# Eight sums of squares in a decoder layer: one plain float32 product each, or two products of rounded parts

## The reference

```python
def rmsnorm(x, g):
    xf = x.astype(jnp.float32)
    y = xf * lax.rsqrt(jnp.mean(xf * xf, axis=-1, keepdims=True) + EPS)
    return (y * g.astype(jnp.float32)).astype(x.dtype)
...
mixed = jnp.sum(gates * proj, axis=2) @ w_mix_out[l]
x = x + rmsnorm(mixed, norm_post_mix[l])
h = rmsnorm(x, norm_pre_xa[l])
mem_n = rmsnorm(mem, mem_norm_g[l])
xa = cross_attention(h, mem_n, xa_wq[l], xa_wkv[l], xa_wo[l])
x = x + rmsnorm(xa, norm_post_xa[l])
h = rmsnorm(x, norm_pre_mlp[l])
ff = jnp.square(jax.nn.relu(h @ mlp_w1[l])) @ mlp_w2[l]
x = x + rmsnorm(ff, norm_post_mlp[l])
```

## Time and profile before

| what | us |
|---|---|
| median of 3 runs (lowest, highest) | 2530.48 (2529.13, 2532.38) |
| the profiled execution, its own time | 2537.36 |
| its span, first to last instruction | 2535.4 |
| busy: PE | 2490.1 (98%) |
| busy: DVE | 1527.9 (60%) |
| busy: POOL | 1240.2 (49%) |
| busy: ACT | 575.6 (23%) |

### The profile page before, as it was taken

One profiled execution on the slowest core, in us unless ns is written; L12 is line 12 of the kernel. 1 busy time (PEld: TensorE's weight loads), 2 busy tenths in 40 slices (PEclk: granted clock), 3 DMA queues, 4 the chain that ended last, 5 costly groups with the idle time before them and its releaser, 6 DMA issues.

```text
span 2535.4 us, 31059 instructions
## 1 busy us (share of the span) xinstructions
PE 2490.1 (98%) x11454; PEld 2053.9 (81%) x11454; DVE 1527.9 (60%) x1618; ACT 575.6 (23%) x777; POOL 1240.2 (49%) x957
## 2 busy tenths in 40 slices
PE   8999999999999999999999999999999999999997
PEld 5788888788888888888778787788788888888885
DVE  6896577587777776699586746652871231622123
ACT  4100444422222222111122214243431110211001
POOL 0433333322222222333676677745776666766663
PEclk9999999999999999999999999999999999999999
DMA  6322121211111112333664344432532232432323
GB/s 236 125 75 79 62 81 60 74 34 44 48 41 42 49 50 100 116 141 108 233 223 143 131 142 161 156 116 67 174 108 95 96 100 94 164 93 98 100 92 115
DMA packets 84883, 270.11 MB, mean 107 GB/s; under 512 B 7888, under 2 KB 9168, under 8 KB 83792
## 3 DMA queue, kind: packets, MB, share of 16 engines
q1 hardware_dynamic: 71760, 244.03, 28.1%
q10 hardware_dynamic: 13056, 25.17, 2.8%
HBM read 224.60 MB, written 44.56 MB: 106 GB/s over the span
## 4 chain that ended last, share of the span: by engine, by line
PE 86%; DVE 6%; issue 3%; POOL 2%; DMA 2%; ACT 2%; SPq 0%; ACTq 0%; POOLq 0%; DVEq 0%
PE ps L369 25%; PE ps L371 25%; PE ps L370 25%; PE xb L510 2%; PE ps L433 1%; POOL w_lo L1911 1%; DVE macc L770 1%; PE ps L423 1%; DMA w_raw<-wall 1%; POOL w_hi L1909 1%; PE xb L533 1%; PE xa L546 1%; PE xb L536 0%; PE xa L524 0%; PE xb L580 0%
## 5 line engine op out<-in xcount | busy, mean ns | idle before, releaser
L1911 POOL TENSOR_TENSOR w_lo<-w_raw,w_hi 128x1024 fp32r<-128x1024 f32 x312 | 791.3, 2536 | 26.0
L1908 POOL TENSOR_TENSOR small<-small 128x1 f32<-128x1 f32 x312 | 88.2, 283 | 1210.7 <-PE ps L371 1009.8
L369 PE MATMUL ps<-h_hi,w_hi 128*128 128x512 f32 x1408 | 559.9, 398 | 1.5 <-ACT sigb L1568 1.3
L371 PE MATMUL ps<-h_hi,w_lo 128*128 128x512 f32 x1408 | 548.7, 390 | 0.0
L370 PE MATMUL ps<-h_lo,w_hi 128*128 128x512 f32 x1408 | 548.4, 389 | 0.0
L369 PE MATMUL ps<-yb_hi,w_hi 128*128 128x512 f32 x1024 | 403.9, 394 | 10.5 <-DVE yb_lo L758 5.7
L371 PE MATMUL ps<-yb_hi,w_lo 128*128 128x512 f32 x1024 | 400.1, 391 | 0.0
L370 PE MATMUL ps<-yb_lo,w_hi 128*128 128x512 f32 x1024 | 400.1, 391 | 0.0
L1909 POOL TENSOR_SCALAR w_hi<-w_raw 128x1024 fp32r<-128x1024 f32 x312 | 356.7, 1143 | 0.0
L369 PEld LDWEIGHTS ps<-h_hi,w_hi 128*128 128x128 f32 x1408 | 264.7, 188 | 56.9 <-issue 3.1
L371 PEld LDWEIGHTS ps<-h_hi,w_lo 128*128 128x128 f32 x1408 | 264.3, 188 | 55.8
(11 more groups left out here) (272 smaller groups left out, 2863.6 us busy)
## 6 DMA issues: line engine op xcount, KB each, us to landing
w_raw<-wall SPq DMA_DIRECT2D x312, 512.0 KB, 3.5
gst<-gate_d SPq DMA_DIRECT2D x24, 512.0 KB, 4.4
w_kv<-wall SPq DMA_DIRECT2D x16, 512.0 KB, 3.6
x_d<-xx ACTq DMA_DIRECT2D x16, 512.0 KB, 3.1
gate_d<-sigb SPq DMA_DIRECT2D x12, 512.0 KB, 2.6
gate_d<-gbuf SPq DMA_DIRECT2D x12, 512.0 KB, 2.8
xs_xa<-x_d ACTq DMA_DIRECT2D x12, 512.0 KB, 4.9
x_sb<-xT SPq DMA_DIRECT2D x2, 2048.0 KB, 15.1
```

Of the source, the lines that this page charges most:

```text
L369: nc.tensor.matmul(out, wh, xh, start=start, stop=False)
L371: return nc.tensor.matmul(out, wl, xh, start=False, stop=stop)
L1908: nc.gpsimd.tensor_tensor(small[:, 13:14], small[:, 12:13], small[:, 12:13], ALU.add)
L1911: nc.gpsimd.tensor_tensor(w_lo[:, u], w_raw[:, u], w_hi[:, u].bitcast(F32), ALU.subtract).then_inc(w_split, 1)
```

## The change

The eight post and pre sums of chains 0 to 3 are no longer one product of `ones` with the float32 `nacc`. ACT rounds `nacc` to `nacc_hi` (in the memory of `rn`), DVE subtracts it to get `nacc_lo` (in place of `nacc`), and PE makes two `fp32r` products with `ones`, summed in PSUM (`parts_total`). PE now waits for `nacc_split`, which the subtraction raises. The rounding stands at the head of `norm_root` on ACT, the subtraction at the head of `root` on DVE. `ones` becomes an `fp32r` tile, written by a cast at the start; all other sums read it as float32.

```diff
-        ones = at("ones", 512, [P, P])
+        ones = at("ones", 512, [P, P], F32R)
...
+        ones_f = at("ones_f", ARENA + 19 * ROW, [P, P])
...
+        nacc_hi = [at(f"nacc_hi{h}", ARENA + 19 * ROW + h * HROW, [P, HALF], F32R) for h in range(2)]
+        nacc_lo = [at(f"nacc_lo{h}", ARENA + 18 * ROW + h * HROW, [P, HALF], F32R) for h in range(2)]
...
+            def parts_total(h, q):
+
+                pe.wait_ge(nacc_split[h], q)
+                nc.tensor.matmul(stat[h], ones[:], nacc_hi[h][:], start=True, stop=False)
+                nc.tensor.matmul(stat[h], ones[:], nacc_lo[h][:], start=False, stop=True).then_inc(nstat_done[h], 1)
+
             def post_stat(c):
 
                 h, q = c % 2, 2 * (c // 2) + 1
+                if c < 4:
+                    parts_total(h, q)
+                    return
                 pe.wait_ge(nacc_ready[h], q)
-                if c < 4:
-                    nc.tensor.matmul(stat[h], ones[:], nacc[h][:], start=True, stop=True).then_inc(nstat_done[h], 1)
-                    return
...
             def pre_stat(c):
 
                 h, q = c % 2, 2 * (c // 2) + 2
-                pe.wait_ge(nacc_ready[h], q)
-                nc.tensor.matmul(stat[h], ones[:], nacc[h][:], start=True, stop=True).then_inc(nstat_done[h], 1)
+                parts_total(h, q)
...
-            v.memset(ones[:], 1.0)
+            done(v.memset(ones_f[:], 1.0))
+            v.tensor_copy(ones[:], ones_f[:])
...
             def root(c, q):
 
                 h = c % 2
+                if c < 4:
+                    dve.wait_ge(nacc_hi_done[h], q)
+                    low(nacc_lo[h][:], nacc[h][:], nacc_hi[h][:]).then_inc(nacc_split[h], 1)
                 dve.wait_ge(nrt_done[h], q)
                 done(newton(rn[h][:], nacc[h][:], stat[h], 1.0 / D))
...
             def norm_root(c, q):
                 h = c % 2
+                if c < 4:
+                    act.wait_ge(nacc_ready[h], q)
+                    copy(nacc_hi[h][:], nacc[h][:]).then_inc(nacc_hi_done[h], 1)
                 act.wait_ge(nstat_done[h], q)
                 rsqrt(rn[h][:], nacc[h][:], stat[h], 1.0 / D).then_inc(nrt_done[h], 1)
```

More of the change, by code:

```diff
@@ L342, in build @@
         nacc_ready, nstat_done, nrt_done = sems("nacc_ready"), sems("nstat_done"), sems("nrt_done")
+        nacc_hi_done, nacc_split = sems("nacc_hi_done"), sems("nacc_split")
         xs_loaded = sems("xs_loaded", 4)
@@ L440, in _ @@
             pe.wait_ge(mem_acc_done, 1)
-            nc.tensor.matmul(xa[:, 0:M], ones[:], m_acc[:], start=True, stop=True).then_inc(mem_stat, 1)
+            nc.tensor.matmul(xa[:, 0:M], ones[:].bitcast(F32), m_acc[:], start=True, stop=True).then_inc(mem_stat, 1)
             for n in range(1, KB):
@@ L447, in _ @@
                 cols = slice(n * HALF, (n + 1) * HALF)
-                mm = nc.tensor.matmul(xb[:, cols], ones[:], x_acc[:, cols], start=True, stop=True)
+                mm = nc.tensor.matmul(xb[:, cols], ones[:].bitcast(F32), x_acc[:, cols], start=True, stop=True)
             mm.then_inc(x_stat, 1)
@@ L545, in head_stat @@
                     cols = slice(n * HALF, (n + 1) * HALF)
-                    mm = nc.tensor.matmul(xa[:, cols], ones[:], hg["osq"][:, cols], start=True, stop=True)
+                    mm = nc.tensor.matmul(xa[:, cols], ones[:].bitcast(F32), hg["osq"][:, cols], start=True, stop=True)
                 mm.then_inc(hstat_done, 1)
@@ L612, in all_tokens_sum @@
                     cols = slice(n * HALF, (n + 1) * HALF)
-                    mm = nc.tensor.matmul(xa[:, cols], ones[:], acc[:, cols], start=True, stop=True)
+                    mm = nc.tensor.matmul(xa[:, cols], ones[:].bitcast(F32), acc[:, cols], start=True, stop=True)
                 mm.then_inc(done, 1)
@@ L626, in _ @@
                         all_tokens_sum(crs, cvar_ready, KB, cvar_mm)
+            def parts_total(h, q):
+                pe.wait_ge(nacc_split[h], q)
+                nc.tensor.matmul(stat[h], ones[:], nacc_hi[h][:], start=True, stop=False)
+                nc.tensor.matmul(stat[h], ones[:], nacc_lo[h][:], start=False, stop=True).then_inc(nstat_done[h], 1)
             def post_stat(c):
                 h, q = c % 2, 2 * (c // 2) + 1
+                if c < 4:
+                    parts_total(h, q)
+                    return
                 pe.wait_ge(nacc_ready[h], q)
-                if c < 4:
-                    nc.tensor.matmul(stat[h], ones[:], nacc[h][:], start=True, stop=True).then_inc(nstat_done[h], 1)
-                    return
-                nc.tensor.matmul(stat[h], ones[:], nacc[h][:], start=True, stop=False)
+                nc.tensor.matmul(stat[h], ones[:].bitcast(F32), nacc[h][:], start=True, stop=False)
                 pe.wait_ge(ysq_done, KB * (h + 1))
-                nc.tensor.matmul(stat[h], ones[:], sqm[:, 1], start=False, stop=True).then_inc(nstat_done[h], 1)
+                nc.tensor.matmul(stat[h], ones[:].bitcast(F32), sqm[:, 1], start=False, stop=True).then_inc(nstat_done[h], 1)
             def pre_stat(c):
                 h, q = c % 2, 2 * (c // 2) + 2
-                pe.wait_ge(nacc_ready[h], q)
-                nc.tensor.matmul(stat[h], ones[:], nacc[h][:], start=True, stop=True).then_inc(nstat_done[h], 1)
+                parts_total(h, q)
             def half_stage(n0, hi, lo, c=None):
```

## The result

The median of four runs is 2555.0 us (2552.64 to 2560.08), against 2531.43 (2529.13 to 2533.12, four runs) for the kernel before: a ratio of 1.0093, 95% interval 1.0078 to 1.0107, or +23.6 us. The prediction was 2551.5 (2541 to 2558), slower. The profiled execution after took 2554.51 us, with a span of 2552.7 and a mean clock of 0.993.

A forecast was written before the change was run, and what follows sets the result against it. PE was taken to bound the kernel (busy 2490.1 us, 98%). Products -3.4, pre-sum waits +18.4 and clock +6.0 gave +21.0 us, which on the median of 2530.5 made 2551.5 us, range 2541 to 2558.

The forecast's parts named there:

- PE bound, every wait counts: Whole kernel: PE busy 2490.1 us, 98% of the span, so each microsecond PE is spared or waits moves the end.
- The products, -3.4: PE at the eight sums: two rounded products take 0.45 us, a plain sum 0.88; 0.43 saved eight times, 3.4 us.
- The post sums, no wait: Four post sums: subtraction done before PE comes; at chain 1 between 0 and 0.4 us of wait, taken as 0.
- The pre sums, 18.4: Four pre sums: PE waits for subtractions behind its last tile, 4.9, 2.5, 4.9 and 6.1 us for chains 0 to 3.
- The tie at chain 1: End of chain 1: DVE's subtraction nearly ties with POOL's `w_lo`; DVE first taken, 2.5 us wait, otherwise 4.9.
- The clock, 6.0: Low clock after the four pre-sum waits: 1.7 us for each long one, half for the short; between 0 and 9.6.
- Faster: Rival at the pre sums: subtractions done before PE arrives, only the 3.4 us saving left, 2527 us; chance 0.03.
- No hold-up by POOL: Rival at ends of chains 0 and 2: subtractions take 0.69 us, PE 2.9 late, not 4.9; 2546 us; chance 0.15.
- the clock hardly answers: Rival after the pre-sum waits: no low-clock cost, +15 without the 6.0, 2546 us; chance 0.14.

The follow-up runs named there:

- experiment 2: Against experiment 1: the subtraction for the post sum of chain 1 also moved, ahead of the token roots of chain 0; 2528.16 us, ratio 0.9994.
- experiment 7: Changed kernel, but each sum is one plain product of `nacc_hi` alone, the low part left out; 2554.72 us, ratio 1.0099.
- experiment 8: Against experiment 2: the Newton step's first result written to the PSUM bank of the sum; 2527.26 us, ratio 0.999.
- experiment 9: Kernel before, plain products, with only the Newton step's first result written to PSUM; 2534.03 us, ratio 0.9988.
- experiment 5: Changed kernel, with PE filling its waits at the four pre sums with products nobody reads; 2547.28 us, ratio 1.0062.
- experiment 1: Changed kernel, with rounding and subtraction for the four pre sums moved ahead of the work on the last tile; 2529.86 us, ratio 0.9998.
- experiment 6: Changed kernel, with the sum left in PSUM so the subtraction has one input in SBUF; 2551.55 us, ratio 1.0087.
- experiment 4: Changed kernel, but only the four pre sums are made from rounded parts, the post sums plain; 2552.01 us, ratio 1.0083.
- kernel 10: Experiment 8 run once more, unchanged, beside experiment 9; 2532.32 us, ratio 0.9993.
- kernel 11: Against experiment 8: the factor `crs` in the convolution module's norm kept in PSUM; 2525.91 us, ratio 0.9975.
- kernel 12: Kernel before, with only the factor `crs` in the convolution module's norm kept in PSUM; 2529.1 us, ratio 0.9991.
- kernel 3: Changed kernel, but only the four post sums are made from rounded parts, the pre sums plain; 2531.73 us, ratio 1.0008.

## Why the prediction was right, by its steps

- *PE bound, every wait counts.* Right: the waits and the low clock together are the loss, +23.3 us of stretch against +21.0 forecast.
- *The products, -3.4.* Mis-sized: **-1.5**. The 0.43 us for each pair was about right (0.40), and at the four pre sums it arrives. "This is certain by the rows, and it is the whole gain" was not: at the four post sums it turns into waits for `w_lo`. The missed step is to ask what PE, earlier by 0.4 us, runs into: the next `w_lo`, which does not come earlier, since POOL and the DVE chain beside it hold each other back (experiments 2, 7, 8 and 9; the Newton step accounts for a third of it, the rest lies behind it).
- *The post sums, no wait.* Right in the changed kernel; at chain 1 the subtraction ended at 1583.45 and PE came at 1585.30, held back by the low clock. Without the low clock (experiment 5) the subtraction ends at 1584.97 and PE comes at 1585.02, again without a wait, so the 0 was right there too. The 0.96 us of experiment 1 belong to another order, with the pre sum on time.
- *The pre sums, 18.4.* Right in place and order, measured 4.5, 2.2, 4.5 and 5.7, **17.0** in all. Most of the difference is the same thing four times: PE starts 0.05 or 0.06 us after DVE's end (1576.88 to 1576.94), not the 0.34 taken from one other wait. The subtraction ended 0.55 us after POOL, as forecast, and experiment 6 shows that it was POOL.
- *The tie at chain 1.* DVE came first by 0.16 us, as chosen, and by 0.15 to 0.16 in the kernels of experiments 4 to 7 as well; so it was close, but it came out the same way in all five traces.
- *The clock, 6.0.* Low: **7 to 8** (experiment 5 and the ledger). The three long waits were priced at 1.7 each, from the row after a wait of 1.93 us, though the only row near 5 us had cost 2.4; by the ledger they cost 2.4, 1.7 and 2.1. The shortest wait, counted by half, cost as much as that at chain 2; the two stretches behind the waits that end at 1577 and 1919 are the long ones.
- *The rivals.* "Faster" would need the subtraction to issue before the last tile ends. That is what experiment 1 builds, and it removes the loss. "No hold-up by POOL" is experiment 6 and "the clock hardly answers" is experiment 5; made true, they take 4 and 7 us off the stretch. For the first the prediction had 5.6, because it let the clock give back 1.6 as well, and that it did not do.

With the measured sizes the sum is 17.0 + 8.0 - 1.5 = 23.5 us. The forecast came as near as it did partly by luck: waits that were 1.4 us too long made up for some of the 1.9 us too much for the products and the 2.0 too little for the clock.

## What to carry to other kernels

When a product's input is split or converted on another engine, look at the place of the new instruction in that engine's order, not at its length: four subtractions of 0.69 us cost 23 us behind the work on the last tile and nothing ahead of it. Where DVE runs beside a POOL that is often busy with SBUF tiles (49% of the span here), keep one input of each DVE instruction on the critical chain in PSUM; here that took 2.55, 1.70 and, for two instructions, 4.33 us down to 0.69, 0.69 and 1.27. And a saving on the bound engine counts only as far as the next buffer it waits for comes earlier too.

## What the runs showed of the hardware

- A DVE instruction of 128x512 with two SBUF tiles as inputs that issues during POOL's `w_lo` ends 0.55 us after it, however early it issued (durations 1.17, 1.31, 1.70, 2.31, 2.55). This also holds for the form with a scalar and two tensors (line 776). One of 128x1024 ends 1.08 or 1.09 us after it (line 782 in kernel 8).
- A wait of 2.0 us was followed by the clock of 1.2 GHz (1630 to 1633, 0.50), one of 2.52 us at 504 in the same execution was not (1.00); but after the wait of 2.56 us at that place in experiment 4's kernel it was 0.58 over the window from 504 to 508, with 3.4 us of it low. The wait of 2.01 us at chain 1 goes both ways too: 0.50 behind it in the changed kernel, 1.00 in experiment 4's. So a wait of 2.0 to 2.6 us may cost nothing or about 1.7 us, and the same place differs from one execution to another.
- The times of the kernel before fall into a group near 2529 and one near 2536 us. The upper one goes with a race between DVE and POOL: the three profiled executions with the wait of 5.2 us (before, kernels 9 and 10) took 2532 to 2537 us, and kernels 11 and 12, without the race, have no such group. It does not explain every slow execution: the profiled one of kernel 3 took 2533.58 us without that wait. On one chip most runs of the kernel before are in the upper one (17 of 23 above 2534), and a change of 0.1% is judged wrongly if the medians mix them. Why a chip prefers one group stays open.
